# Suffix sums of a stick-breaking attention from strip totals, and four reorderings, in a two-layer decoder kernel

## What is computed

```python
def block(args):                                   # 128 queries, all keys
    z = jnp.einsum('bhqd,bhkd->bhqk', qblk, kf) * scale
    log_1m = jnp.where(strict, jax.nn.log_sigmoid(-z), 0.0)
    suffix = lax.cumsum(log_1m, axis=3, reverse=True) - log_1m
    a = jnp.where(strict, jnp.exp(jax.nn.log_sigmoid(z) + suffix), 0.0)
    return jnp.einsum('bhqk,bhkd->bhqd', a, vf)
...
out = (softmax(q1 k1^T) - lam * softmax(q2 k2^T)) v      # layer B, then rms_norm, silu(gate), w_out
```

## Time and profile before

| | us |
|---|---|
| median of 3 runs | 661.46 (661.09 to 663.24) |
| profiled execution, its own time | 661.75 |
| span in that execution | 660.5 |
| TensorE busy in the span | 628.2 |
| VectorE, GpSimd, ScalarE busy | 443.5, 352.2, 336.3 |
| pairs of layer A in the span | 79.3 to 311.9 |
| heads of layer B in the span | 454.6 to about 632 |

### The profile page before, as it was taken

How to read it: one execution, slowest core, us unless ns; L and a number is a source line. 1 busy time by engine, 2 the same in 40 slices (tenths; PEclk the granted TensorE clock), 3 DMA queues, 4 the chain that set the end, 5 groups by cost and what they waited for, 6 DMA issues and landing times.

```text
span 660.5 us, 9992 instructions
## 1 busy us (share of the span) xinstructions
PE 628.2 (95%) x3324; PEld 528.0 (80%) x3324; DVE 443.5 (67%) x701; ACT 336.3 (51%) x728; POOL 352.2 (53%) x339
## 2 busy tenths in 40 slices
PE   5899999999999999989999999999899999969998
PEld 4788778888888888868877888788788888867876
DVE  3484197977969688593336398425979999966531
ACT  5342366674857657574326534323565565545320
POOL 4665595564555645183542455457765557733261
PEclk9999999999999999999999999999899999979999
DMA  7432131212211111022110222232322222121041
GB/s 253 108 112 82 50 110 50 65 48 64 64 48 48 51 61 62 0 82 77 66 64 34 96 96 95 82 106 62 87 65 73 55 79 80 41 72 33 32 160 64
DMA packets 61773, 49.08 MB, mean 74 GB/s; under 512 B 7728, under 2 KB 48816, under 8 KB 61744
## 3 DMA queue, kind: packets, MB, share of 16 engines
q1 hardware_dynamic: 58064, 48.25, 23.7%
q10 hardware_dynamic: 3680, 0.46, 0.5%
HBM read 44.50 MB, written 2.10 MB: 71 GB/s over the span
## 4 chain that ended last, share of the span: by engine, by line
PE 63%; DVE 21%; ACT 6%; issue 5%; POOL 3%; DMA 1%; DVEq 0%; SPq 0%; ACTq 0%; POOLq 0%
PE bank L582 16%; PE bank L583 15%; PE bank L584 15%; PE bank L696 6%; DVE hi L1452 4%; PE bank L710 3%; DVE sp L1446 2%; DVE lo L1457 2%; ACT pr L1289 2%; PE bank L681 2%; POOL w_lo L477 1%; ACT ex L1106 1%; DVE small L1646 1%; DMA xs<-in_x 1%; DVE h_hi L1414 1%
## 5 line engine op out<-in xcount | busy, mean ns | idle before, releaser
L477 POOL TENSOR_TENSOR w_lo<-w_raw,w_hi 128x512 fp32r<-128x512 f32 x100 | 146.1, 1461 | 8.0
L465 POOL TENSOR_TENSOR w_lo<-w_raw,w_hi 128x512 fp32r<-128x512 f32 x60 | 82.2, 1377 | 114.9 <-ACT w_hi L993 114.9
L475 POOL CAST w_hi<-w_raw 128x512 fp32r<-128x512 f32 x100 | 72.4, 724 | 130.0 <-PE bank L584 53.1
L582 PE MATMUL bank<-w_hi,h_hi 128*128 128x512 f32 x320 | 127.9, 400 | 6.9 <-POOL w_lo L477 3.0
L582 PE MATMUL bank<-h_hi,w_hi 128*128 128x512 f32 x320 | 131.0, 409 | 2.6 <-ACT q L1205 2.6
L583 PE MATMUL bank<-h_lo,w_hi 128*128 128x512 f32 x320 | 126.8, 396 | 0.0
L584 PE MATMUL bank<-h_hi,w_lo 128*128 128x512 f32 x320 | 126.8, 396 | 0.0
L584 PE MATMUL bank<-w_hi,h_lo 128*128 128x512 f32 x320 | 125.1, 391 | 0.0
L583 PE MATMUL bank<-w_lo,h_hi 128*128 128x512 f32 x320 | 124.9, 390 | 0.0
L582 PEld LDWEIGHTS bank<-w_hi,h_hi 128*128 128x128 f32 x320 | 60.1, 188 | 21.5 <-POOL w_lo L477 4.3
L582 PEld LDWEIGHTS bank<-h_hi,w_hi 128*128 128x128 f32 x320 | 61.0, 191 | 17.1 <-ACT q L1205 2.5
(11 more groups left out here) (174 smaller groups left out, 1201.5 us busy)
## 6 DMA issues: line engine op xcount, KB each, us to landing
w_raw<-in_a_w_in SPq DMA_DIRECT2D x64, 256.0 KB, 2.8
w_raw<-in_w_kv SPq DMA_DIRECT2D x32, 256.0 KB, 3.1
w_raw<-in_b_w_in SPq DMA_DIRECT2D x32, 256.0 KB, 2.8
w_raw<-in_a_w_out SPq DMA_DIRECT2D x16, 256.0 KB, 2.6
w_raw<-in_b_w_out SPq DMA_DIRECT2D x16, 256.0 KB, 3.0
xs<-in_x SPq DMA_DIRECT2D x4, 512.0 KB, 5.2
qrot<-qs SPq DMA_DIRECT2D x32, 64.0 KB, 2.0
out_x<-xs SPq DMA_DIRECT2D x8, 256.0 KB, 2.7
```

Of the source, the lines that this page charges most:

```text
L465: nc.gpsimd.tensor_tensor(w_lo[s][:, :], w_raw[s][:, :], w_hi[s][:, :].bitcast(F32), ALU.subtract).then_inc(s_w, 1)
L475: nc.gpsimd.tensor_copy(w_hi[s][:, :], w_raw[s][:, :]).then_inc(s_whi, 1)
L477: nc.gpsimd.tensor_tensor(w_lo[s][:, :], w_raw[s][:, :], w_hi[s][:, :].bitcast(F32), ALU.subtract).then_inc(s_w, 1)
L582: pe.matmul(o, ahi, bhi, start=start, stop=False, skip_group_check=True)
```

## The change

1. Suffix sums. The strips get a new layout (`STRIP_A`: banks of 512, 384 and 256+128 columns). A product with `neg_one` is made with the first 128 columns of the next strip, and one with totals that VectorE has added up: `totals` makes three blocks of 128 columns with two additions (256 and 128 columns, in `osum`), `totals_split` splits them (a cast and a subtraction of 384 columns, `tot_hi`, `tot_lo`). 16 matmuls for a head in place of 20, with 768 columns of `neg_one` in place of 1280 for each of hi and lo, all behind the four triangle products. The wait for the totals (`s_stl`) stands ahead of the first product that uses them.
2. The suffix sums stand one projection step later in both places.
3. GpSimd: in pairs 1 to 5 the first slab split waits for the totals of head 0, the second for those of head 1; in pair 6 the first waits for head 0's.
4. In pair 6 the slabs G_OUT to G_OUT+3 are split ahead of the values of pair 7.
5. `cor` is gone (`og` takes its place), and `keep_output` of pair p-1 moves from the end of that pair to pair p, behind the second `totals_split` and ahead of `gate_log`.
6. Head 6: the sums move to after the fourth step of the second gate projection. ScalarE squares the output right after the two copies; VectorE makes the gate ahead of the addition to q.
7. Head 0: the third q is copied two exponentials sooner.

```diff
+STRIP_A = {0: (0, 512), 1: (512, 384), 2: (896, 256), 3: (1152, 128)}
+BANKS_A = [(0, 512), (512, 384), (896, 384)]
+BANK_STRIPS_A = [[0], [1], [2, 3]]
...
         with pool.Fori(1, KT - 2) as i:
             values_a(i)
+            pool.wait_ge(s_stl, i * 2 + 1)
             for j in range(6):
+                if j == 1:
+                    pool.wait_ge(s_stl, i * 2 + 2)
                 split(G_BODY + 6 + j, i, 6)
         values_a(KT - 2)
+        pool.wait_ge(s_stl, (KT - 2) * 2 + 1)
         split(G_GLAST)
         split(G_GLAST + 1)
+        for g in range(G_OUT, G_OUT + 4):
+            split(g)
         values_a(KT - 1)
-        for g in range(G_OUT, N_A):
+        for g in range(G_OUT + 4, N_A):
...
         def suffix_sums(p, h):
+            def add(j, i, w, moving, n):
+                c = STRIP_A[j][0] - BANKS_A[b][0] + (i - j) * P
+                for part in moving:
+                    mm = pe.matmul(bank[3 * h + b][:, cols(c, n)], w[:, :], part, start=False, stop=False,
+                                   skip_group_check=True)
+                return mm
...
             pe.wait_ge(s_sl, p * 6 + (3 * h + 3))
             for b in range(3):
-                for j in BANK_STRIPS[b]:
-                    for i in range(j, TT):
...
+                for j in BANK_STRIPS_A[b]:
+                    mm = add(j, j, neg_tri, strips(j, STRIP_A[j][1]), STRIP_A[j][1])
+            for b in range(3):
+                j = b
+                mm = add(j, j + 1, neg_one, strips(j + 1, P), P)
+                if b < 2:
+                    pe.wait_ge(s_stl, p * 2 + (h + 1))
+                    mm = add(j, j + 2, neg_one, totals(2 * P * b, 2 * P - b * P), 2 * P - b * P)
                 mm.then_inc(s_t, 1)
...
-            project(G_BODY + 2, h1_hi, h1_lo, bank[7][:, :], p, 6, between=lambda: suffix_sums(p, 0))
+            project(G_BODY + 2, h1_hi, h1_lo, bank[7][:, :], p, 6, between=lambda: suffix_sums(p, 0), after=4)
-            project(G_BODY + 4, h1_hi, h1_lo, bank[6][:, :], p, 6, between=lambda: suffix_sums(p, 1), after=0)
+            project(G_BODY + 4, h1_hi, h1_lo, bank[6][:, :], p, 6, between=lambda: suffix_sums(p, 1), after=1)
...
         attend_before(h, 2)
-        sums(h + 1, h - 1)
+
+        def sum_and_turn_last():
+            sums(h + 1, h - 1)
+            turn_probs(h)
+
-        project(H_GATES + 2, h1_hi, h1_lo, bank[6][:, :], between=lambda: turn_probs(h))
+        project(H_GATES + 2, h1_hi, h1_lo, bank[6][:, :], between=sum_and_turn_last)
...
+                if b == 1 and first:
+                    q_copy(h + 3, q_used)
-            if q_used is not None:
+            if q_used is not None and not first:
                 q_copy(h + 3, q_used)
             if later is not None and h == KT - 2:
-                gate_parts(h, later)
+                gate_copies(h, later)
+                output_square(h - 1)
             if q_next:
                 act.wait_ge(s_z, h * 6 + 54)
                 q_round(h + 1)
-            if not first:
+            if later is not None and h == KT - 2:
+                gate_log(h + (KT + 1))
+            elif not first:
                 output_square(h - 1)
...
+            def totals(h):
+                s, tot = sp[h], osum
+                dve.wait_ge(s_sp, p * 6 + (3 * h + 3))
+                def pieces(v, c, step):
+                    return v[:, c:c + step + P].rearrange("p (a n) -> p a n", n=P)[:, 0:step // P + 1:step // P, :]
+                TTN(pieces(tot, 0, 2 * P), pieces(s, 640, 384), pieces(s, 896, 256), ALU.add).then_inc(s_st, 1)
+                dve.wait_ge(s_st, p * 4 + (2 * h + 1))
+                TTN(tot[:, cols(P, P)], s[:, cols(768, P)], tot[:, cols(2 * P, P)], ALU.add).then_inc(s_st, 1)
+
+            def totals_split(h):
+                dve.wait_ge(s_st, p * 4 + (2 * h + 2))
+                if h:
+                    dve.wait_ge(s_t, p * 6 + 3)
+                V.tensor_copy(tot_hi[:, :], osum[:, 0:384]).then_inc(s_sth, 1)
+                dve.wait_ge(s_sth, p * 2 + (h + 1))
+                TTN(tot_lo[:, :], osum[:, 0:384], tot_hi[:, :].bitcast(F32), ALU.subtract).then_inc(s_stl, 1)
...
             soft_hi(2)
+            totals(0)
             soft_lo(2)
+            totals_split(0)
             soft(3)
...
             soft_hi(5)
+            totals(1)
             soft_lo(5)
+            totals_split(1)
+            if not first:
+                keep_output(p - 1, p)
             gate_log(p + 1)
             weights_lo(0)
...
             combine((3, 2), 2, 4)
+            if silu_first:
+                gate_silu(h + KT)
             if q_next:
                 q_add(h + 2)
-            if gate:
+            if gate and not silu_first:
                 gate_silu(h + KT)
```

More of the change, by code:

```diff
@@ L682, in scores_a, with strips, totals @@
                                            q[rows, j * P:SEQ], start=False, stop=False, skip_group_check=True)
-                            if j == BANK_STRIPS[b][-1] and step == 2:
+                            if j == BANK_STRIPS_A[b][-1] and step == 2:
                                 mm.then_inc(s_z, 1)
         def suffix_sums(p, h):
+            def add(j, i, w, moving, n):
[4 more added lines that the diff above has]
+                return mm
+            def strips(i, n):
+                return [part[h][:, cols(STRIP_A[i][0], n)] for part in (hi, lo)]
+            def totals(at, n):
+                return [part[:, cols(at, n)] for part in (tot_hi, tot_lo)]
             pe.wait_ge(s_sl, p * 6 + (3 * h + 3))
             for b in range(3):
-                for j in BANK_STRIPS[b]:
-                    for i in range(j, TT):
[L693 to L698, removed]
+                for j in BANK_STRIPS_A[b]:
+                    mm = add(j, j, neg_tri, strips(j, STRIP_A[j][1]), STRIP_A[j][1])
[5 more added lines that the diff above has]
+                    mm = add(j, j + 2, neg_one, totals(2 * P * b, 2 * P - b * P), 2 * P - b * P)
                 mm.then_inc(s_t, 1)
@@ L1155, in correction @@
             if not first:
-                act.wait_ge(s_os, p * 2 + (h - 1))
+                act.wait_ge(s_o, p)
             main, other = slice(DH * h, DH * h + DH), slice(DH - DH * h, P - DH * h)
-            A(cor[main, :], o[other, :], ACT.Copy).then_inc(s_cor, 1)
+            A(og[main, :], o[other, :], ACT.Copy).then_inc(s_cor, 1)
         pair(0, first=True)
@@ L1430, in sum_output @@
             dve.wait_ge(s_cor, p * 2 + (h + 1))
-            TTN(osum[main, :], o[main, :], cor[main, :], ALU.add).then_inc(s_os, 1)
+            TTN(osum[main, :], o[main, :], og[main, :], ALU.add).then_inc(s_os, 1)
         def finish(p, o0, o1):
@@ L1439, in finish, with pair @@
             TTN(og[:, :], osum[:, :], silu[:, :], ALU.mult).then_inc(s_og, 1)
-            keep_output(p, p + 1)
-        def pair(p, last=False):
+        def pair(p, first=False, last=False):
             def soft(m):
-                seg = cols(*BANKS[m % 3])
+                seg = cols(*BANKS_A[m % 3])
                 dve.wait_ge(s_ln, p * 6 + (m + 1))
-                STT(out=sp[m // 3][:, seg], in0=bank[m][:, 0:BANKS[m % 3][1]], scalar=0.0, op0=ALU.max,
+                STT(out=sp[m // 3][:, seg], in0=bank[m][:, 0:BANKS_A[m % 3][1]], scalar=0.0, op0=ALU.max,
                     in1=ex[m // 3][:, seg], op1=ALU.add).then_inc(s_sp, 1)
             def soft_hi(m):
-                seg = cols(*BANKS[m % 3])
+                seg = cols(*BANKS_A[m % 3])
                 dve.wait_ge(s_sp, p * 6 + (m + 1))
@@ L1544, in _ @@
             V.tensor_copy(v32[:, n % TT, cols(HALF, HALF)], bank[n % 6][:, :]).then_inc(s_vkd, 1)
-        pair(0)
+        pair(0, first=True)
         with dve.Fori(1, KT - 1) as i:
@@ L1549, in _ @@
         finish(KT - 1, bank[0], bank[3])
+        keep_output(KT - 1, KT)
         def add_residual(g, m, half, banks_of=range(8)):
@@ L1634, in o_times_gate, with head @@
                 op1=ALU.mult).then_inc(s_ot, 1)
-        def head(h, n_before, q_next=True, q_after=True, gate=True):
+        def head(h, n_before, q_next=True, q_after=True, gate=True, silu_first=False):
             def biases(v, b):
@@ L1712, in _ @@
             st.leave(KT - 4)
-        head(KT - 2, 2, q_after=False)
+        head(KT - 2, 2, q_after=False, silu_first=True)
         gate_log(2 * KT - 1)
```

30 lines of the change are left out of this document (18 added, 12 removed).

## The result

The changed kernel takes 668.9 us (median; 667.2 to 672.0), the kernel before 662.4 beside it (661.1 to 663.6): a ratio of 1.0104, with a 95% interval of 1.0059 to 1.0150. It is slower by 1.0%, some 7 us, and the interval leaves out no change. 663.0, no clear change, was forecast; the range of 649 to 671 holds the result. The profiled execution took 667.17 us, its span is 665.9.

A forecast was written before the change was run, and what follows sets the result against it. TensorE, busy 95% of the span, was taken as the bound, other engines counting only where it waits. 661.75 + 8.8 (layer A) - 7.2 (head 6) - 0.2 (head 0) = 663.1, given as 663.0 us; eight in ten: 649 to 671.

The forecast's parts named there:

- Turns: Of two SBUF-to-SBUF instructions of VectorE and GpSimd, the later waits for the earlier; those reading PSUM are free of it.
- The replay: Pair 2 replayed on its own clock for pairs 1 to 5: waits of 1.5 and 1.7 us before `attend_a`, +1.6 a pair.
- Products: Suffix sums: fewer `neg_one` columns save 0.5 us a head, 8 us in all; the wait for `lo` goes as well.
- Pair 0: Not held, so new instructions wait for turns; TensorE's waits grow from 1.5 to some 5 us: +2.3 us (0 to +4).
- rival 2: Slower: the clock falls at the end of each of six pairs, some 1.6 us each: 673 us; chance 0.10.
- Pair 6: Only the first slab is held, head 1's chain is hindered and end waits stay: +2.2 us (-1.6 to +4).
- Pair 7: Early output slabs remove 3.0 us of waits; the last two slabs delay VectorE's first chain: -3.7 us (-2.5 to -4.5).
- Head 6: Layer B: idle falls from 4.95 to 1.3 us, half clock goes, 0.4 back at head 7's gate: -7.2 us.
- Head 0: Layer B: third q comes 1.1 us sooner, but `turn_probs` waits for VectorE: -0.2 us (+1.5 to -0.3).
- Rival 1: The pair's tail has room, `q_lo` and `k_lo` come in time: 644 us, or 653 if half goes; chance 0.27.
- Rival 3: Head 6 gives half, as the clock falls all the same or `ot` is late: 667 us; chance 0.13.
- Rival 4: Layer A's waits and products stay about as before; only head 6, head 0 and pair 7's waits gain: 651; chance 0.08.

The follow-up runs named there:

- run 1: The changed kernel with each pair's output split (`keep_output`) back at the end of its own pair: 658.0 us, ratio 0.9917 to the kernel before.
- run 4: run 1's kernel with GpSimd's second hold moved: from a pair's third slab on it waits for head 0's low weights: 655.8 us, ratio 0.9863.
- run 2: The changed kernel with GpSimd's holds taken out: 684.5 us, ratio 1.0290 to the kernel before.
- run 7: run 4's kernel with the same two holds in pair 0, output slabs held in pair 6 and the sixth until pair 7's first totals: 645.6 us, ratio 0.9738.
- run 8: The kernel before with GpSimd holds alone, its 20 matmuls a head without totals: 660.4 us, ratio 0.9953.
- run 6: The kernel before with only the first four output slabs split early, in pair 6 ahead of pair 7's values: 660.0 us, ratio 0.9941.
- run 3: The changed kernel without GpSimd's holds and with the output split at the end of its own pair: 666.4 us, ratio 1.0066 to the kernel before.
- run 5: The kernel before with the changes to head 6 alone: 658.3 us, ratio 0.9932.

## Why the prediction was right or wrong, point by point

- **Turns: right, and it was the step that decided.** The replay gave 8.2 us from the release to `q_lo`; the trace has 8.3. It gave waits of 1.5 and 1.7 us before `attend_a`; they are 1.25 and 1.41 in pair 2. The forecast of +1.6 a pair came to +1.75. On the forecast's own clock for pair 2 (3.92 us earlier, by the starts of the scores), the totals are split at 146.6 and 153.0 (146.75 and 153.0 forecast), `q_lo` ends at 161.9 (161.8) and `k_lo` at 165.6 (165.5). Taking away one link of that chain (run 1) or the GpSimd halves in it (run 4) moved the time as turns demand. The Trainium skill states SBUF interfaces shared by VectorE and GpSimd, with contention (GPSIMD Engine Reference, Specifications). The traces agree: in run 2 the cast of 384 columns takes 0.35 us alone and 1.45 behind a GpSimd subtraction, and `soft`, `q_lo` and `k_lo`, which read PSUM, stay within 0.02 us of their least at one size.
- **Products: the size was off.** I put 0.5 us a head; runs 7 and 8 give 0.36. The floor of a pair, 26.7, is 26.9. The wait that should go did go. In pairs 1 to 5 this error didn't reach the sum: TensorE came to `attend_a` 0.4 us later than forecast and waited that much less, since VectorE's chain set the pair's end.
- **Pair 0: +2.3 forecast, +3.0 measured, by another way.** I expected the waits at the sums to grow from 1.5 to some 5 us. They came to 2.3 (2.06 and 0.22), and the second sums did not wait. But half clock followed from 92.9 to 99.8: 6.9 us that do the work of 3.5, a loss of 3.4. This is the mechanism of rival 2, in a place where I had not put it. That the two numbers lie near each other is luck.
- **Pair 6: right** (+2.2, measured +2.3): waits of 0.73 and 0.24 at the second sums, 1.80 for `k_lo`.
- **Pair 7: -3.7 forecast, -2.5 measured.** The slabs were there, as run 6 confirms alone (-3.1). But half clock at 290.9 to 294.3, just behind pair 6's wait of 1.80, made the scores 3.36 us long in place of 2.19. These 1.2 us are the size of the miss.
- **Head 6: -7.2 forecast, -5.6 measured.** The idle stretch fell to 1.14 (1.3 forecast) and the half clock went: 7.8 us together, 7.6 forecast. Mis-sized is what comes late next: I allowed 0.4 us for the gate of head 7; TensorE waits 0.27 at the masks and 1.22 at the first tile, and with the restarts behind the waits the masks and the scores of head 7 take 2.2 us longer than before.

```profile
594.67 0.47 PE L597 MATMUL bank<-h_hi,w_hi 128*128 128x512 f32 x1 [1.14 <-ACT g L1110]
...
604.08 0.38 PE L677 MATMUL bank<-mask_b,ident_r 128*128 128x256 f32 x1 [0.27 <-DVE at_lo L1765]
608.08 0.47 PE L597 MATMUL bank<-w_hi,h_hi 128*128 128x512 f32 x1 [1.22 <-ACT g L1110]
```

- **Head 0: -0.2 forecast, 0 in the trace** (19.8 us from one head's scores to the next in both). The mechanism was right: the wait for the third q fell from 2.07 to 0.98 us, and the half clock that followed it before (466.1 to 469.6) didn't come. All of it went into new waits for VectorE, 1.19 us ahead of `turn_probs` and 0.41 and 0.27 at the masks, and the restarts behind them. It was not tried alone.
- **Rivals.** Rival 1 (the tail has room) is false for this order, and true once the output's split is out of it and GpSimd is held: pairs 1 to 6 of run 7 take 26.9 us, near the 26.7 that it asked for. Rival 2 asked for half clock in each of six pairs; waits of 1.25 and 1.41 brought none in pairs 1 to 5, the wait of 1.80 in pair 6 did. It was nearer than it looks: the waits of 1.77 to 1.80 in run 2 were followed by half clock in four pairs of five. The case that I weighed it by, pair 7's waits of 1.27 and 1.06 at full clock, was one outcome of two: in run 8 half clock came with the same two waits (1.27 and 1.04). Rival 3 (667) lies nearest to the measured time, but not by its cause: head 6 gave 5.6 us, not half, and its clock did not fall. Rival 4 is false, as runs 1 to 3 show.
- **The sum.** The forecast of no clear change is wrong, and its own range of 659.5 to 667 leaves out 668.9; it is the wider range that holds. The mechanism was right and sizes were off: forecast 8.8 - 7.2 - 0.2 = +1.4, measured between the profiled executions +5.4. The 4.0 us between are 1.9 in pairs 0 and 7 (both behind half clock), 0.7 in pairs 1 to 5, 0.1 in pair 6, 1.6 in head 6 and 0.2 in head 0, less the 0.9 by which layer A begins earlier; 0.4 are spread. The medians differ by 6.6 us, 1.2 more than these two executions. Of the four executions of the changed kernel the two faster ones (667.2 and 668.0) show a granted clock of 0.992 over the whole, the two slower ones (669.8 and 672.0) 0.990. A mean clock lower by 0.002 is worth some 1.3 us, so more time at half clock is likely a part of it; no trace of those two is there to show it.

## What to carry to other kernels

Where two engines take turns, moving work is a question of whose turn it lengthens: first list which results TensorE asks for next, then keep the other engine's free work away from exactly those. Work taken from the bottleneck is worth nothing while a chain elsewhere ends later; run 7 does the same work as the changed kernel and is 23 us faster by four holds more, one placed later and one call put back. And look behind every wait for the clock: the wait of 2.06 us in pair 0 was followed by half clock that cost 3.4.

## What the runs showed of the hardware

**Turns.** In layer A of the changed kernel VectorE's instructions that read PSUM vary little (`soft` of 512 columns 0.68 to 0.69 us, `k_lo` 0.68 to 0.69), while those that read SBUF alone reach 1.1 us more than their least as soon as GpSimd splits a slab beside them (`lo` of 384 columns 0.55 to 1.65, the cast of 512 0.43 to 1.07). GpSimd's cast goes from 0.61 to 1.17.

**Half clock** (1.2 in place of 2.4 GHz) did not follow each wait alike, and the length of the wait alone does not tell. The same wait in the same place, with its outcome:

| wait of TensorE | half clock behind it | none |
|---|---|---|
| first sums of pair 0, 2.05 to 2.06 us, then a shorter one at the totals | the change (92.9 to 99.8), runs 1 and 3 | runs 2 and 4; it came there behind the next wait, 1.98 and 1.99 |
| `k_lo`, 1.77 to 1.80 | pair 6 of the change, four pairs of run 2 | one pair of run 2 |
| slabs in pair 7, 1.26 to 1.27, then 1.04 to 1.07 | run 8 | the kernel before, run 5 |
| third q in head 0, 2.07 to 2.08 | the kernel before, runs 5 and 6 | run 8 |

It did not come behind 1.25 and 1.41 in pairs 1 to 5 of the changed kernel, with 2.2 us of matmuls between them, behind 1.5 in five pairs of run 3, nor behind 1.19 in run 7. It did come behind 1.24 in head 0 of run 3. The third row, as stretches of run 8 and of the kernel before:

```profile
289.30:292.70 3.40, 2.81 (x7) 2.32 (x8) 3.37 (x6) 0.00 (x0) 3.32 (x4) 0.50 0.35 127
289.30:292.70 3.40, 2.34 (x11) 1.64 (x10) 3.37 (x6) 0.63 (x1) 3.24 (x4) 1.00 0.42 119
```

What tells the cases apart stays open. At half clock twelve matmuls of head 6's projection took 5.1 us (590.97 to 596.07 in the kernel before), at full clock 2.8 (594.67 to 597.50 in the changed kernel). So a difference of 1 or 2 us between two single executions can be the clock and no part of the change.
